# A two-layer block on one core: VectorE reads the first unit of an output-weight chunk before it makes the low part of the coming weights

## The chip, the core and the metric

The kernel runs on one core of a Trainium2 chip. The metric is the device time of one execution in microseconds, and a time for a kernel is the median of several executions. The engines are named as in the profile: PE (TensorE, matrix products), DVE (VectorE), ACT (ScalarE), POOL (GpSimd) and SP (SyncE, which here issues the loads).

## What is computed

Two blocks of two layers each are run on 256 tokens of width 1024, all in float32. Only the first block is touched. One of its layers, cut to what matters:

```python
hdn = modulate(rmsnorm(x, norm1_g[l]), shift1, scale1)
proj = hdn @ w_in[l]            # queries, keys, values of three branches, and gates
...
g_a, g_b, g_c = jnp.split(jax.nn.sigmoid(gates), N_BRANCH, axis=-1)
merged = (g_a * (o_mla @ w_o_mla[l]) + g_b * (o_sb @ w_o_sb[l])
          + g_c * (o_mb @ w_o_moba[l]))
x = x + gate1[:, None, :] * (merged @ w_out[l])
hdn = modulate(rmsnorm(x, norm2_g[l]), shift2, scale2)
ff = jnp.square(jax.nn.relu(hdn @ w_ff1[l])) @ w_ff2[l]
x = x + gate2[:, None, :] * ff
```

The three products with `w_o_sb`, `w_o_moba` and `w_o_mla` (512 x 1024 each) are what this case is about. "Output weights" means these three.

## The kernel before

**Chunks and steps.** The weights of a layer are cut into 76 chunks of up to 128 x 2048 numbers. Each engine runs one loop over the chunks (`for j in range(N_CHUNKS)`), and one turn of it is a step. The output weights have two chunks each: steps 26 and 27 (`WSB`, first branch), 32 and 33 (`WMB`, second), 38 and 39 (`WMLA`, third). Four steps of gate columns stand ahead of each pair, and steps 40 to 43 (`WOUT`) follow the last.

**Split weights.** Products are made in float32 accuracy from two parts of each operand. ScalarE makes the high part of a chunk (`split_high`, line 539, tile `w_hi`), VectorE subtracts it from the weights for the low part (`split_low`, line 545, tile `w_lo`), and TensorE does three matmuls for each pair of tiles (lines 1644, 1646 and 1648). There are two buffers for each part (`SPLIT = 2`), so in step j the chunk for step j + 2 is split, in two halves. ScalarE may write the first half once TensorE is through with the first half of the old chunk (`half_used`), and the second half once the chunk is used up (`unit_done`). The raw weights are loaded by SP into a ring of three; the load of the chunk three further waits for the low part's second half (`lo_made`).

**Units and banks.** The result of a chunk is one unit, in one of two PSUM banks (`dense`), which take turns. An output-weight chunk has two units, one for each half of its columns, with 24 matmuls each. In `products` of such a chunk, `half_used` is signalled in the second unit, at its half, hence after three quarters of the step's 48 matmuls. Before TensorE starts a unit it waits until the bank's unit before is read (`bank_of`, semaphores `evacuated`).

**Reading a unit.** VectorE multiplies a unit of an output-weight chunk by its gate (line 2209), into `merged` (tile `first_full`) for the first branch and into `gated` (tile `first_sq`) for the others. GpSimd adds `gated` to `merged` (line 2093). In the third branch ScalarE then takes the high part of the sum (line 2072) and VectorE the low part (line 2265), and the chunks of `WOUT` need both (`merged_ready`, in four pieces).

**Order on VectorE.** In a step VectorE does the attention work that is due, then the low part's first half, then `evacuate(j)`, then the low part's second half, then what is particular to the step. `split_ahead` makes the halves; for output-weight chunks each call makes one half. Instructions of an engine run in the order of its queue, and an instruction that waits holds back all behind it.

Of the kernel before, what the change touches and what calls it, by code (L numbers as in the profile page):

```python
# [13 lines left out]
ALU = mybir.AluOpType  # L14
# [34 lines left out]
GB, WSB, GC, WMB, GA, WMLA, WOUT, FF = 22, 26, 28, 32, 34, 38, 40, 44  # L49
# [76 lines left out]
def is_down(j):  # L126
    return j >= FF and FF_STEPS[j - FF][0] == "down"


def is_out(j):  # L130

    return WSB <= j < GC or WMB <= j < GA or WMLA <= j < WOUT


def units_of(j):

    if is_down(j):
        return 0
    if j == UKV:
        return 6  # L140
    return 2 if is_out(j) else 1
# [4 lines left out]
RING = [sum(units_of(i % N_CHUNKS) for i in range(g)) for g in range(DEPTH * N_CHUNKS + 1)]  # L146
DONE = [sum(max(1, units_of(i % N_CHUNKS)) for i in range(g)) for g in range(DEPTH * N_CHUNKS + 1)]
# [15 lines left out]
def constants_first():  # L163
# [16 lines left out]
    for j in range(4):  # L180
        k[32 * j, K_SEL + j] = 1.0
        for v in range(2):
# [20 lines left out]
                    gate_ready=12, merge_added=8, merged_hi=4, merged_ready=4, ff_hi_made=16, ff_ready=16,  # L203
# [44 lines left out]
def reach(engine, counted, n):  # L248
    engine.wait_ge(counted.sem, counted.left + n)
# [29 lines left out]
def layers(nc, a, keep, out):  # L279
    with ExitStack() as stack:  # L280
        m = Memory(nc, stack, "first")
# [18 lines left out]
        merged = full  # L300
        gated = sq
# [15 lines left out]
        gate = m.sb("gate", [P, KT, S])  # L317
# [31 lines left out]
        dense = [m.bank(f"dense{i}") for i in range(2)]  # L349
# [19 lines left out]
        evacuated = [m.sem(f"evacuated{i}") for i in range(2)]  # L369
# [6 lines left out]
        hi_made, lo_made, half_used, unit_done = (m.sem(n) for n in ("hi_made", "lo_made", "half_used", "unit_done"))  # L376
# [88 lines left out]
        def half_columns(g, half):  # L465

            nk, nc_ = shape_of(g % N_CHUNKS) if g < DEPTH * N_CHUNKS else (KT, CW)
            n = nk // 2 * nc_
            return slice(half * n, half * n + n)

        def split_ahead(split, g, half):


            if g < DEPTH * N_CHUNKS:
                early = half_columns(g + SPLIT, 0).stop <= half_columns(g, 0).stop and units_of(g % N_CHUNKS) <= 2
                if half and not early:
                    split(g + SPLIT, 0)
                if half or early:
                    split(g + SPLIT, half)
# [14 lines left out]
        def folds_at(at):  # L494
            return [unit for step, unit, _ in FOLDS if step == at]
# [5 lines left out]
        def groups_at(at, lag):  # L501
            return [n for n, g in enumerate(GROUPS) if GROUP_END[g] + lag == at]
# [5 lines left out]
        def pair_stage(j):  # L508

            return [(n, s) for s in (2, 1, 0) for n, at in enumerate(PAIR_STEP) if at + s * PAIR_LAG == j]  # L510
# [6 lines left out]
        for j in range(MBQ, MBV):  # L517
            t = mb_q if j < MBK else mb_k
# [1095 lines left out]
        def layer(l, next_x_ready):  # L1614

            base = l * N_CHUNKS
# [11 lines left out]
            gate_ready, merge_added, merged_hi, merged_ready = (  # L1628
                Counted(first_sems[n], FIRST_COUNTS[n] * l) for n in ("gate_ready", "merge_added", "merged_hi", "merged_ready"))
# [465 lines left out]
            def vector(dve, link):  # L2095
# [45 lines left out]
                def rope(j):  # L2141

                    t, lo, hi, kind, swap = ropes[j]
                    n, no = t.shape[1], rope_no[j]
                    wait_evacuated(dve, RING[base + j])
                    other = swapped[lo:hi, 0:n, :]
                    dve.stream_shuffle(other, t, swap).then_inc(rope_swapped.sem, 1)
                    reach(dve, rope_swapped, no + 1)
                    dve.tensor_tensor(other, other, table(kind, 1, lo, hi, n), ALU.mult)
                    link(dve.tensor_tensor(t, t, table(kind, 0, lo, hi, n), ALU.mult))  # L2150
                    dve.tensor_tensor(t, t, other, ALU.add).then_inc(rope_done.sem, 1)
                    reach(dve, rope_done, no + 1)
# [37 lines left out]
                def after_values(n):  # L2190
# [2 lines left out]
                    dve.tensor_tensor(o_lo[n // 4][:, n % 4, :], o_bank[:, 0:S], o.bitcast(F32),  # L2193
                                      ALU.subtract).then_inc(o_ready.sem, 1)

                def evacuate(j):
                    if j in ropes:
                        rope(j)
                    elif is_out(j):
                        first = {WSB: 0, WMB: 1, WMLA: 2}[j - j % 2]  # L2200
                        reach(dve, gate_ready, 4 * first + 4)
                        for e in range(2):
                            t, u = 4 * (j % 2) + 2 * e, RING[base + j] + e
                            dve.wait_ge(unit_done, DONE[base + j] + e + 1)
                            if first == 2:

                                reach(dve, merge_added, t // 2 + 1)
                            dst = gated if first else merged
                            dve.tensor_tensor(dst[:, t:t + 2, :], gate[:, t:t + 2, :],  # L2209
                                              dense[u % 2][:].rearrange("p (m t) -> p m t", m=2),  # L2210
                                              ALU.mult).then_inc(evacuated[u % 2], 1)
                    elif WOUT <= j < FF:
                        u = RING[base + j]
                        dve.wait_ge(unit_done, DONE[base + j] + 1)
                        residual(2 * (j - WOUT), dense[u % 2], 16).then_inc(evacuated[u % 2], 1)
                    elif j in UP_NO:
                        n, (_, q, c) = UP_NO[j], FF_STEPS[j - FF]
                        reach(dve, ff_hi_made, n + 1)
                        dve.tensor_tensor(ff_lo[q % 2][:, 2 * c:2 * c + 2, :], relu_sq[n % 2],
                                          ff_hi[q % 2][:, 2 * c:2 * c + 2, :].bitcast(F32),  # L2220
                                          ALU.subtract).then_inc(ff_ready.sem, 1)
                    elif is_down(j) and FF_STEPS[j - FF][1] == 3:
                        c = FF_STEPS[j - FF][2]
                        dve.wait_ge(unit_done, DONE[base + j + 1])
                        last = residual(2 * c, acc[c], 40)
                        last.then_inc(next_x_ready, 1)

                def residual(t, bank, gate_at):

                    for c in range(2):  # L2230
                        last = dve.scalar_tensor_tensor(
                            out=keep.x[:, t + c, :], in0=bank[:, c * S:(c + 1) * S],
                            scalar=mod[:, gate_at + t + c:gate_at + t + c + 1], in1=keep.x[:, t + c, :],
                            op0=ALU.mult, op1=ALU.add)
                    return last
# [10 lines left out]
                for j in range(N_CHUNKS):  # L2246
                    if j == FF:
                        norm_x(1, NORM2)
                    for n, stage in pair_stage(j):
                        (after_scores, after_second, after_values)[stage](n)  # L2250
                    for n in groups_at(base + j, SELECT_LAG):
                        keep_group(dve, n)
                    if j == WOUT:
                        dve.wait_ge(group_kept, GROUPS.index((l, "ada", 1)) + 1)
                    split_ahead(partial(split_low, dve), base + j, 0)
                    evacuate(j)
                    split_ahead(partial(split_low, dve), base + j, 1)
                    for i, at in enumerate(LAT_STEP):
                        if at <= j <= at + 2:
                            (latent_root, latent_scale, latent_low)[j - at](NORM_Q + i)  # L2260
                    if WMLA <= j < WOUT:
                        for e in range(2):
                            t = 4 * (j - WMLA) + 2 * e
                            reach(dve, merged_hi, 2 * (j - WMLA) + e + 1)
                            dve.tensor_tensor(h_lo[:, t:t + 2, :], merged[:, t:t + 2, :],
                                              h_hi[:, t:t + 2, :].bitcast(F32), ALU.subtract).then_inc(
                                                  merged_ready.sem, 1)
                    for unit in folds_at(base + j):
                        fold(dve, unit)
                    if l == DEPTH - 1:  # L2270
                        turn_vector(dve, link, j - FF, low_free)
# [5 lines left out]
        first = layer(0, later[-1]["x_ready"].sem)  # L2277
# [328 lines left out]
```

## Time and profile before

| | |
|---|---|
| median of 3 runs | 1500.1 us (1499.57 to 1501.39) |
| profiled execution, its time | 1500.05 us |
| profiled execution, its span from the first to the last instruction | 1498.2 us |
| PE busy | 1422.3 us (95%) |
| DVE busy | 839.3 us (56%) |
| ACT busy | 756.0 us (50%) |
| POOL busy | 146.2 us (10%) |
| mean granted clock of TensorE | 0.987 |

The profile is of one execution. Busy times are those of an engine's instructions; matmuls are pipelined and their ends are modelled, so they overlap each other. What counts for an engine that is nearly always busy is where it stands still, and what ended the wait.

### The profile page before, as it was taken

How to read it: one execution, taken by the hardware profiler on the slowest of the kernel's cores; microseconds unless marked ns; L12 is line 12 of the kernel's file. 1: busy time of each engine (PE TensorE's matmuls, PEld its weight loads, DVE VectorE, ACT ScalarE, POOL GpSimd, SP SyncE). 2: the span in 40 equal slices, each digit the busy share in tenths (PEclk: the TensorE clock that was granted, in tenths of full speed). 3: DMA queues.
4: the chain of work that ended last, by engine and by line, in shares of the span. 5: the costliest groups of instructions: out<-in, count | busy, mean ns of one | idle time of the engine just before them, and what ended most of it. 6: DMA issues, size and time to landing. Idle time of an engine off the chain costs nothing.

```text
span 1498.2 us, 25346 instructions
## 1 busy us (share of the span) xinstructions
PE 1422.3 (95%) x10680; PEld 1284.6 (86%) x10680; DVE 839.3 (56%) x1274; ACT 756.0 (50%) x1229; POOL 146.2 (10%) x78
## 2 busy tenths in 40 slices
PE   6999999998999998999899989999999999999988
PEld 2989878988899998998798988999998778688978
DVE  3547855546666566568845565534463635517562
ACT  3465555654545434565565554644553455425562
POOL 0000000011000000000000110000002333133321
PEclk9999999999999999999999999999999999999999
DMA  9854556454788795642755455876543221122330
GB/s 358 334 177 155 173 184 226 141 196 142 253 295 305 269 330 179 208 141 73 268 173 172 154 184 194 317 269 198 159 151 94 85 84 59 55 92 87 114 113 29
DMA packets 196292, 269.31 MB, mean 180 GB/s; under 512 B 7117, under 2 KB 175954, under 8 KB 189906
## 3 DMA queue, kind: packets, MB, share of 16 engines
q1 hardware_dynamic: 196178, 267.68, 52.4%
q8 instruction: 85, 1.39, 0.4%
q14 instruction: 29, 0.24, 0.1%
HBM read 266.61 MB, written 1.05 MB: 179 GB/s over the span
## 4 chain that ended last, share of the span: by engine, by line
PE 77%; DVE 13%; ACT 5%; issue 2%; SPq 1%; DMA 1%; DVEq 0%; ACTq 0%
PE first_dense L1644 12%; PE first_dense L1646 12%; PE first_dense L1648 12%; PE first_dense L1002 5%; PE first_dense L1005 5%; PE first_dense L1004 5%; DVE first_w_lo L545 3%; PE first_misc L228 2%; PE first_s L1644 2%; PE first_s L1646 2%; PE first_s L1648 2%; PE first_dense L1822 2%; PE first_o L1644 1%; ACT first_w_hi L539 1%; PE first_t L1644 1%
## 5 line engine op out<-in xcount | busy, mean ns | idle before, releaser
L545 DVE TENSOR_TENSOR first_w_lo<-first_raw,first_w_hi 128x1024 fp32r<-128x1024 f32 (+2 forms) x308 | 370.5, 1210 | 329.6 <-ACT first_w_hi L539 328.0
L539 ACT ACTIVATE first_w_hi<-first_raw 128x1024 fp32r<-128x1024 f32 (+2 forms) x308 | 314.9, 1029 | 273.4 <-PE first_dense L1648 128.5
L1644 PE MATMUL first_dense<-first_h_parts,first_w_hi 128*128 128x256 f32 x1312 | 376.8, 287 | 10.4 <-DVE first_sq L2209 6.5
L1646 PE MATMUL first_dense<-first_h_parts,first_w_hi 128*128 128x256 f32 x1312 | 372.5, 284 | 0.0
L1648 PE MATMUL first_dense<-first_h_parts,first_w_lo 128*128 128x256 f32 x1312 | 372.3, 284 | 0.0
L1644 PEld LDWEIGHTS first_dense<-first_h_parts,first_w_hi 128*128 128x128 f32 x1312 | 252.4, 192 | 24.0 <-issue 13.6
L1646 PEld LDWEIGHTS first_dense<-first_h_parts,first_w_hi 128*128 128x128 f32 x1312 | 252.5, 192 | 0.1
L1648 PEld LDWEIGHTS first_dense<-first_h_parts,first_w_lo 128*128 128x128 f32 x1312 | 252.5, 192 | 0.0
L702 POOL TENSOR_TENSOR first_w_lo<-first_raw,first_w_hi 128x1024 fp32r<-128x1024 f32 x41 | 100.6, 2455 | 451.3 <-ACT first_w_hi L695 451.3
L1004 PE MATMUL first_dense<-first_parts,first_w_hi 128*128 128x512 f32 (+1 forms) x384 | 130.8, 341 | 0.0
L1002 PE MATMUL first_dense<-first_h_parts,first_w_hi 128*128 128x512 f32 (+1 forms) x320 | 112.1, 350 | 0.9 <-DVE first_w_lo L702 0.9
L1005 PE MATMUL first_dense<-first_h_parts,first_w_lo 128*128 128x512 f32 (+1 forms) x320 | 109.4, 342 | 0.0
L1644 PE MATMUL first_dense<-first_parts,first_w_hi 128*128 128x256 f32 (+1 forms) x320 | 93.5, 292 | 10.0 <-ACT first_area L2012 6.5
L1648 PE MATMUL first_dense<-first_parts,first_w_lo 128*128 128x256 f32 (+1 forms) x320 | 92.1, 288 | 0.0
L1646 PE MATMUL first_dense<-first_parts,first_w_hi 128*128 128x256 f32 (+1 forms) x320 | 91.9, 287 | 0.0
L695 ACT ACTIVATE first_w_hi<-first_raw 128x1024 fp32r<-128x1024 f32 x56 | 59.0, 1056 | 60.5 <-PE first_dense L1005 60.5
L1004 PEld LDWEIGHTS first_dense<-first_parts,first_w_hi 128*128 128x128 f32 x384 | 72.8, 190 | 9.0 <-issue 1.2
L1644 PEld LDWEIGHTS first_dense<-first_parts,first_w_hi 128*128 128x128 f32 (+1 forms) x320 | 60.3, 188 | 17.6 <-issue 10.6
L1644 PE MATMUL first_s<-first_parts,first_w_hi 128*128 128x256 f32 x256 | 73.0, 285 | 0.0
L1002 PEld LDWEIGHTS first_dense<-first_h_parts,first_w_hi 128*128 128x128 f32 x320 | 60.6, 189 | 14.3 <-issue 7.8
L1646 PE MATMUL first_s<-first_parts,first_w_hi 128*128 128x256 f32 x256 | 72.4, 283 | 0.0
L1648 PE MATMUL first_s<-first_parts,first_w_lo 128*128 128x256 f32 x256 | 72.4, 283 | 0.0
(391 smaller groups left out, 2795.3 us busy)
## 6 DMA issues: line engine op xcount, KB each, us to landing
first_raw<-in_w_in SPq DMA_DIRECT2D x78, 1024.0 KB, 5.1
first_raw<-in_w_ff SPq DMA_DIRECT2D x64, 1024.0 KB, 6.4
first_units<-in_w_ada SPq DMA_DIRECT2D x41, 1024.0 KB, 6.4
first_raw<-in_w_out SPq DMA_DIRECT2D x16, 1024.0 KB, 5.1
first_mb<-in_w_mod SPq DMA_DIRECT2D x14, 1024.0 KB, 7.2
first_units<-in_w_mod SPq DMA_DIRECT2D x10, 1024.0 KB, 5.9
first_raw<-in_w_uq SPq DMA_DIRECT2D x8, 576.0 KB, 3.9
first_raw<-in_w_o_sb SPq DMA_DIRECT2D x4, 1024.0 KB, 4.9
```

Source lines behind the costliest of these rows:

```text
L228: product = pe.matmul(out[32 * j:32 * j + 32, :], c[:, t, :], moving, start=first, stop=last, skip_group_check=True)
L539: act.activation(w_hi[g % SPLIT][:, c], raw[g % CHUNK_RING][:, c], ACT.Copy).then_inc(hi_made, 1)
L545: dve.tensor_tensor(w_lo[g % SPLIT][:, c], raw[g % CHUNK_RING][:, c], w_hi[g % SPLIT][:, c].bitcast(F32), ALU.subtract).then_inc(lo_made, 1)
L695: act.activation(in_tiles(w_hi[place2(l, c, SPLIT)][:])[:, r, :], in_tiles(raw[place2(l, c, CHUNK_RING)][:])[:, r, :], ACT.Copy).then_inc( ...
L702: engine.tensor_tensor(in_tiles(w_lo[place2(l, c, SPLIT)][:])[:, r, :], in_tiles(raw[place2(l, c, CHUNK_RING)][:])[:, r, :], hi.bitcast(F3 ...
L1002: pe.matmul(out, still[0](t), moving[0](t), start=t == i == 0, stop=False, skip_group_check=True)
L1004: pe.matmul(out, still[0](t), moving[1](t), start=False, stop=False, skip_group_check=True)
L1005: last = pe.matmul(out, still[1](t), moving[0](t), start=False, stop=t == KT - 1, skip_group_check=True)
L1644: pe.matmul(out, still[0](t), moving[0](t), start=start and t == n == 0, stop=False, skip_group_check=True)
L1646: pe.matmul(out, still[0](t), moving[1](t), start=False, stop=False, skip_group_check=True)
L1648: last = pe.matmul(out, still[1](t), moving[0](t), start=False, stop=stop and t == nk - 1, skip_group_check=True)
L1822: pe.matmul(at[i][:, c, :], part[:, t, c * P:(c + 1) * P], h_hi[:, t, :], start=part is w[i][0] and t == c == 0, stop=False, skip_group_ch ...
```

## The change

In the steps of output weights the reads of the two units are taken apart. The read of the first unit (`evacuate_out(j, 0)`, with its waits) comes ahead of the low part of the first half of the chunk two steps ahead, and the read of the second unit (`evacuate_out(j, 1)`) stays between the two halves. The rest of `evacuate` is as it was.

```diff
+                def evacuate_out(j, e):
+                    first = {WSB: 0, WMB: 1, WMLA: 2}[j - j % 2]
+                    t, u = 4 * (j % 2) + 2 * e, RING[base + j] + e
+                    reach(dve, gate_ready, 4 * first + 4)
+                    dve.wait_ge(unit_done, DONE[base + j] + e + 1)
+                    if first == 2:
+                        reach(dve, merge_added, t // 2 + 1)
+                    dst = gated if first else merged
+                    dve.tensor_tensor(dst[:, t:t + 2, :], gate[:, t:t + 2, :],
+                                      dense[u % 2][:].rearrange("p (m t) -> p m t", m=2),
+                                      ALU.mult).then_inc(evacuated[u % 2], 1)
+
                 def evacuate(j):
                     if j in ropes:
                         rope(j)
-                    elif is_out(j):
-                        first = {WSB: 0, WMB: 1, WMLA: 2}[j - j % 2]
-                        reach(dve, gate_ready, 4 * first + 4)
-                        for e in range(2):
...
+
+                    if is_out(j):
+                        evacuate_out(j, 0)
                     split_ahead(partial(split_low, dve), base + j, 0)
+                    if is_out(j):
+                        evacuate_out(j, 1)
                     evacuate(j)
                     split_ahead(partial(split_low, dve), base + j, 1)
```

## Rows read from the trace of the kernel before

**Rows 1.** The page, part 1: busy us, share of the span, instructions.

```profile
PE 1422.3 (95%) x10680; PEld 1284.6 (86%) x10680; DVE 839.3 (56%) x1274; ACT 756.0 (50%) x1229; POOL 146.2 (10%) x78
```

**Rows 2.** Line 2209: durations in ns, min/median/max; who waited (us, times).

```profile
L2209 DVE TENSOR_TENSOR first_sq<-first_gate,first_dense x16: 678/680/682, 295.9 to 887.1; 128x512 f32<-128x512 f32 x16
...
  PE first_dense L1644: 8.2, 6
```

**Rows 3.** Timeline of TensorE: start us, duration us, instruction, idle before and releaser.

```profile
259.21 0.39 PE L1644 MATMUL first_dense<-first_h_parts,first_w_hi 128*128 128x256 f32 x1 [0.84 <-DVE first_full L2209]
...
302.37 0.28 PE L1648 MATMUL first_dense<-first_parts,first_w_lo 128*128 128x256 f32 x1
...
304.28 0.39 PE L1644 MATMUL first_dense<-first_h_parts,first_w_hi 128*128 128x256 f32 x1 [1.63 <-DVE first_sq L2209]
...
336.01 0.35 PE L1644 MATMUL first_dense<-first_parts,first_w_hi 128*128 128x256 f32 x1 [1.68 <-issue]
...
343.63 0.39 PE L1644 MATMUL first_dense<-first_h_parts,first_w_hi 128*128 128x256 f32 x1 [1.64 <-DVE first_sq L2209]
...
347.87 0.36 PE L1644 MATMUL first_dense<-first_h_parts,first_w_hi 128*128 128x256 f32 x1 [1.10 <-DVE first_h_parts L2265]
...
701.33 0.80 PE L1785 MATMUL first_o<-first_small,first_area 128*64 128x256 f32 x2 [2.13 <-DVE first_small L2187]
...
891.48 0.36 PE L1644 MATMUL first_dense<-first_h_parts,first_w_hi 128*128 128x256 f32 x1 [1.10 <-DVE first_h_parts L2265]
```

**Rows 4.** Chain of waits, 300 to 306 us: start, us on the chain, what.

```profile
301.31 1.07 ACT first_w_hi L539
...
302.40 0.04 DVE first_w_lo L545
...
303.55 0.69 DVE first_sq L2209
...
304.28 0.39 PE first_dense L1644
```

**Rows 5.** Timeline of VectorE, first and second branch.

```profile
257.34 1.23 DVE L545 TENSOR_TENSOR first_w_lo<-first_raw,first_w_hi 128x1024 fp32r<-128x1024 f32 x1 [4.16 <-ACT first_w_hi L539]
...
302.40 1.23 DVE L545 TENSOR_TENSOR first_w_lo<-first_raw,first_w_hi 128x1024 fp32r<-128x1024 f32 x1 [2.99 <-ACT first_w_hi L539]
```

**Rows 6.** Timelines of VectorE, GpSimd and ScalarE, third branch.

```profile
334.08 1.23 DVE L545 TENSOR_TENSOR first_w_lo<-first_raw,first_w_hi 128x1024 fp32r<-128x1024 f32 x1 [1.25 <-ACT first_w_hi L539]
...
335.99 3.53 POOL L2093 TENSOR_TENSOR first_full<-first_full,first_sq 128x512 f32<-128x512 f32 x2 [28.15 <-DVE first_sq L2209]
...
339.55 0.63 ACT L2072 ACTIVATE first_h_parts<-first_full 128x512 fp32r<-128x512 f32 x1 [1.60 <-POOL first_full L2093]
...
340.21 0.69 DVE L2265 TENSOR_TENSOR first_h_parts<-first_full,first_h_parts 128x512 fp32r<-128x512 f32 x1
...
341.75 1.23 DVE L545 TENSOR_TENSOR first_w_lo<-first_raw,first_w_hi 128x1024 fp32r<-128x1024 f32 x1 [0.85 <-ACT first_w_hi L539]
...
343.65 1.29 POOL L2093 TENSOR_TENSOR first_full<-first_full,first_sq 128x512 f32<-128x512 f32 x1 [4.14 <-DVE first_sq L2209]
...
344.09 1.94 DVE L545 TENSOR_TENSOR first_w_lo<-first_raw,first_w_hi 128x1024 fp32r<-128x1024 f32 x1
...
344.90 2.27 POOL L2093 TENSOR_TENSOR first_full<-first_full,first_sq 128x512 f32<-128x512 f32 x1
...
345.95 1.77 DVE L2265 TENSOR_TENSOR first_h_parts<-first_full,first_h_parts 128x512 fp32r<-128x512 f32 x1
```

**Rows 7.** Stretches: length; busy us and instructions of PE, PEld, DVE, ACT, POOL; PEclk; DMA share; GB/s.

```profile
337.00:348.00 11.00, 8.26 (x67) 7.89 (x66) 9.86 (x9) 4.81 (x7) 6.03 (x4) 1.00 0.38 112
...
450.00:580.00 130.00, 128.27 (x1050) 121.95 (x1050) 82.16 (x72) 59.57 (x71) 0.00 (x0) 1.00 0.85 297
...
586.00:590.00 4.00, 4.00 (x24) 4.00 (x24) 4.00 (x11) 2.50 (x7) 0.00 (x0) 0.62 0.02 6
...
700.00:704.00 4.00, 2.37 (x9) 1.37 (x10) 3.19 (x7) 3.63 (x6) 0.47 (x1) 0.71 0.00 0
```

More of the change, by code:

```diff
@@ L2198, in evacuate @@
                         rope(j)
-                    elif is_out(j):
-                        first = {WSB: 0, WMB: 1, WMLA: 2}[j - j % 2]
-                        reach(dve, gate_ready, 4 * first + 4)
-                        for e in range(2):
[L2203 to L2211, printed above, removed]
                     elif WOUT <= j < FF:
```

## Prediction

> **What bounds the kernel.** The page's first part is read first: TensorE is busy for 1422.3 of 1498.2 us [rows 1], so a change pays only where TensorE stands still. Next comes the list of what line 2209, the read of an output-weight unit, is waited for by: TensorE waited 8.2 us for it, in six pauses [rows 2]. TensorE's timeline then places the pauses. In the first layer they end at 259.21 (0.84 us), 304.28 (1.63), 336.01 (1.68, put down to "issue", but it ends as the first of two reads finishes) and 343.63 (1.64); the second layer repeats them 543.6 us later, as the row at 891.48 does for the one at 347.87 [rows 3]. That last one (1.10 us) waits for the low part of the merged result (line 2265).
>
> The chain of waits through one pause tells its cause. TensorE finishes the third quarter of the step's products; only then may ScalarE take the high part of the first half of the weights two steps ahead (301.31, 1.07 us); VectorE takes the low part (302.40); then it reads the first unit (303.55), and TensorE goes on at 304.28 [rows 4]. The first unit's products had been ready since half of the step. TensorE needs its bank, not the weights, which are for two steps later.
>
> **What the change removes and adds.** No instruction is added or removed, and no DMA. In twelve steps (three pairs in each of two layers) one multiply of 0.68 us [rows 2] goes ahead of one subtraction of 1.23 us. The wait for the gates goes forward too (they are done a step earlier), and in the third branch the wait for the second branch's sums (GpSimd was done with them 28.15 us earlier [rows 6]). The second read keeps its place before the second subtraction, which can start up to 0.68 us earlier; SP's next load of weights waits for that one, and is so no later.
>
> *The wait moved forward.* VectorE now stops at the queue's head for unit one, at half of the step, where it used to stop for ScalarE after three quarters. It stood idle before that subtraction for 4.16 us in the step at 257, 2.99 at 302, 1.25 at 334 and 0.85, the shortest of the twelve, at 341 [rows 5, 6]. So the 0.68 us fits into idle time everywhere and the subtraction keeps its time; that cover is gone only in the step at 341, once TensorE comes earlier (below). Without cover it costs 0.68 us of VectorE, in front of a low part that TensorE wants a step and a half later: nothing on the path.
>
> *Pairs of the first branch (two in the kernel).* The first of their steps is followed by attention work and row products on TensorE, so its bank is free in time either way: 0. The second: VectorE stands idle for 4.16 us ahead of 257.34 [rows 5], in which the unit comes ready and is read, so the bank is free before it is asked for, and the pause of 0.84 us goes but for the usual handover of 0.05: 0.8 us.
>
> *Pairs of the second branch.* In the first step the transposes behind it nearly hide the read; I take 0.15 us (bounds 0 and 0.3). The second step's pause goes whole. A pause counted from a modelled end of a matmul (start 302.37 plus 0.28) is short by what matmuls overlap: they start 0.12 us apart (1050 in 127 to 130 us [rows 7]), so 0.16 is added, and 304.28 moves to 302.49: 1.79 us. The next chunks' low parts are done by then: the second half's was made one step before.
>
> *Pairs of the third branch.* The first step's pause goes: 1.68 + 0.16 = 1.84 us, so the second step starts at 334.17. There a second chain takes over, and I walk it [rows 6]. GpSimd adds each read to the sum (line 2093). Its add takes 1.29 us alone at 343.65, while VectorE reads a bank beside it at no cost; but VectorE's subtraction issued at 344.09 takes 1.94 us instead of 1.23, which is 1.23 us counted from the add's end; GpSimd's next add (344.90) takes 2.27, which is about 1.14 from the subtraction's end; the subtraction of line 2265 issued at 345.95 then takes 1.77 instead of 0.69. So subtractions and adds take turns whole. The Trainium skill, "SBUF — State Buffer", section "Who interferes with whom", states this as a lock: a VectorE instruction with two SBUF inputs and a GpSimd one that reads SBUF block each other for the whole instruction, and one with a single SBUF input doesn't contend; the trace agrees.
>
> With the change the first read comes right behind the work that ends 1.25 us ahead of 334.08: 332.8 to 333.5. The first add starts then, and the subtraction at 334.08 waits for it until 334.7, ending at 335.95. Second read to 336.55, second subtraction (now ahead of the add) to 337.70, add to 338.9, ScalarE's high part to 339.55 (as before), line 2265 to 340.28 instead of 340.90. Then the first read of the second step, 340.20 to 340.88: TensorE, done with that step at 340.15, starts the next chunk at 340.94 instead of 343.63. First subtraction to 342.03, second read to 342.63, add 342.03 to 343.2, second subtraction to 344.35, add to 345.5, line 2265 to 346.05: TensorE passes its last pause at 346.2 instead of 347.87. So of 1.84 + 1.80 + 1.26 us, 1.7 us are gained and the rest is the same wait in a later place. Bounds: if GpSimd's third add gets in ahead of the subtraction at 340.8, 0.9 us later, gain 0.8; if line 2265 gets in ahead of the last add, 1.15 us earlier, gain 2.8. I take 1.7: the subtraction is asked for 0.1 us before the add.
>
> **Sum.** Per layer 0.8 + 0.15 + 1.79 + 1.7 = 4.44 us; two layers 8.9. The profiled execution took 1500.05 us, 1.85 more than its span, and the median of the three runs is 1500.1, the same. 1500.1 - 8.9 = 1491.2 us.
>
> Behind these places everything is released by TensorE's own progress: the feed-forward stretch from 450 to 580 us keeps TensorE busy 128.27 of 130 us with the DMA engines 85% busy [rows 7], and its loads are issued as splits finish, so they move along.
>
> **Rivals.** *The third branch gives nearly all back.* GpSimd and VectorE take turns in the bad order there, and more often than in my walk. For it: requests only 0.1 us apart. Against it: even the bad order, once, leaves 0.8; with half of that, 2 x (0.8 + 0.15 + 1.79 + 0.4) = 6.3, so 1493.8 us. 0.13.
>
> *The clock falls in the longer pause.* The pauses of 1.10 to 1.68 us left the granted clock at 1.00 from 337 to 348 us. The one of 2.13 us that ends at 701.33 [rows 3] was followed by 0.50, which leaves 0.71 as the mean of 700 to 704, and 586 to 590 has 0.62 [rows 7]: half of 2.4 GHz. My new pause before 346.2 is about 2.3 us. A mean of 0.62 over 4 us is 3.0 us at 0.50, so a fall gives back 1.5 us. The Trainium skill, "TensorE: Matmul & The Clock Gate", Part 1, has the clock at only these two levels and lets it fall when the engine has been idle; the trace shows both levels. Once: 1492.7; in both layers: 1494.2. 0.27 together. It can go the other way too, since pauses further on shift and the one at 701 might keep its clock: 1489.7.
>
> *DMA takes it back.* If the feed-forward stretch were paced by the DMA engines, TensorE would wait there for what it gained, and the first layer's 4.4 us would be lost: 1495.7, or 1499 with a like loss in the second. Against it: TensorE's 98.7% there. 0.06.
>
> *Slower: the head of the queue.* If VectorE, stopped for unit one or for the merge before it, delays the low part of weights two steps ahead until TensorE wants it, each of twelve steps pays 0.68 us: 8.2 us, 1508. It decides from the point where the low part is late by more than the step between making and use, over 5.8 us (48 matmuls at 0.12); idle time of 0.85 to 4.16 us in front of it says it is far off. 0.03.
>
> **How the numbers follow.** The sum as forecast has 0.51 (its own range 1490 to 1492.5); the rivals have 0.13, 0.27, 0.06 and 0.03. From 1488.8 (the good order of locks in both layers) to 1495.2 holds all but the DMA rival, the slow one and tails. A measurement of this kernel can tell 0.2%, 3 us, from no change: all cases but the last two are faster by more, and a part of DMA's is the same. Faster 0.92, same 0.05, slower 0.03.
>
> **What would show it.** In the changed profile VectorE's line for the read stands singly, one before each first subtraction; the pauses near 259 and 304 are gone (TensorE's next chunk starts 0.12 us after the last matmul); near 336 none, near 341 one below 1 us, near 344 one of some 2 us on line 2265. GpSimd's first add lies beside the first subtraction, which reads 1.8 us. The granted clock behind that pause decides the clock rival; a new wait of ScalarE for a load, with a pause of TensorE behind it in 380 to 580, the DMA one. I am wrong if TensorE's pauses outside these steps grow by what is gained here.

## The result, and the profile after

| | before | changed |
|---|---|---|
| median of 6 runs each | 1500.02 us (1499.43 to 1501.39) | 1492.39 us (1491.34 to 1496.47) |
| profiled execution: time, span, mean granted clock | 1500.05, 1498.2 us, 0.987 | 1496.47, 1494.7 us, 0.983 |

The ratio is 0.995 with a 95% interval of 0.994 to 0.996: 7.6 us less. The profiled execution of the changed kernel is the slowest of its six, so its own rows add up to 3.6 us. Places along its timeline are therefore compared one by one. They show 7.3 us gained in the touched steps of the two layers, and 1.1 us lost ahead of them, 1.7 between 907 and 917 us, and 1.0 behind 1452.

TensorE's timeline of the changed kernel, at the places of [rows 3]:

```profile
259.35 0.36 PE L1644 MATMUL first_dense<-first_h_parts,first_w_hi 128*128 128x256 f32 x1
...
302.30 0.28 PE L1644 MATMUL first_dense<-first_h_parts,first_w_hi 128*128 128x256 f32 x1
...
338.73 0.39 PE L1644 MATMUL first_dense<-first_h_parts,first_w_hi 128*128 128x256 f32 x1 [0.73 <-DVE first_sq L2204]
...
343.86 0.35 PE L1644 MATMUL first_dense<-first_h_parts,first_w_hi 128*128 128x256 f32 x1 [1.99 <-DVE first_h_parts L2269]
```

The pauses at 259 and 304 are gone, the one at 336 too; 0.73 us stands in place of the 1.64 at 343.63; and the last one, for the merged result's low part, has grown from 1.10 to 1.99 us. Just ahead of the touched steps the times are 1.12 us later than in the profile of before (0.92 of it arises in the first 40 us), so a place's gain is its shift against that: the chunk behind the first branch starts 0.98 us earlier (259.35 for 259.21), the one behind the second branch 3.10 (302.30 for 304.28), and the last pause ends 5.13 earlier (343.86 for 347.87).

VectorE, GpSimd and ScalarE of the changed kernel, third branch (to [rows 6]; line 2204 is the read, line 2269 what was 2265):

```profile
330.66 0.68 DVE L2204 TENSOR_TENSOR first_sq<-first_gate,first_dense 128x512 f32<-128x512 f32 x1
...
331.42 1.30 POOL L2093 TENSOR_TENSOR first_full<-first_full,first_sq 128x512 f32<-128x512 f32 x1 [25.09 <-DVE first_sq L2204]
...
332.00 1.80 DVE L545 TENSOR_TENSOR first_w_lo<-first_raw,first_w_hi 128x1024 fp32r<-128x1024 f32 x1 [0.66 <-ACT first_w_hi L539]
...
334.32 1.21 DVE L545 TENSOR_TENSOR first_w_lo<-first_raw,first_w_hi 128x1024 fp32r<-128x1024 f32 x1
...
334.48 2.21 POOL L2093 TENSOR_TENSOR first_full<-first_full,first_sq 128x512 f32<-128x512 f32 x1 [1.76 <-DVE first_sq L2204]
...
336.72 0.64 ACT L2072 ACTIVATE first_h_parts<-first_full 128x512 fp32r<-128x512 f32 x1 [2.79 <-POOL first_full L2093]
```

The read stands singly ahead of the first subtraction, and GpSimd's first add now lies under that subtraction, which takes 1.80 us. Turn by turn it is the order of the prediction's walk; the walk's times are 2.1 us later at its start and 2.3 us later at its end.

Stretches of the changed kernel (columns as in [rows 7]), behind that last pause in each layer, and one further on:

```profile
344.60:347.60 3.00, 3.00 (x16) 3.00 (x16) 1.23 (x1) 0.17 (x1) 0.00 (x0) 0.50 0.79 269
884.20:887.20 3.00, 3.00 (x16) 3.00 (x16) 1.55 (x2) 0.54 (x1) 0.00 (x0) 0.51 0.86 286
908.00:911.00 3.00, 3.00 (x9) 2.34 (x8) 0.10 (x1) 0.92 (x2) 0.00 (x0) 0.50 0.00 0
```

The granted clock is 0.50 for some 3 us behind the pause of 1.99 us, in both layers: 16 matmuls start in 3 us where the kernel before starts 25 at clock 1.00 in the stretches behind the same wait:

```profile
347.90:350.90 3.00, 3.00 (x25) 3.00 (x26) 1.88 (x2) 0.88 (x1) 0.00 (x0) 1.00 0.95 308
891.50:894.50 3.00, 3.00 (x25) 3.00 (x26) 1.90 (x2) 0.90 (x1) 0.00 (x0) 1.00 0.93 305
```

The next chain, the squares behind `WOUT`, begins at 367.47 for 369.97. Of the 5.13 us, 3.62 are left, so the fall costs 1.51 us; in the second layer it costs 1.46. The third stretch is a fall that the kernel before didn't have there, behind a pause of 1.73 us that follows TensorE's last matmuls of `WOUT`.

### The profile page after: what moved, and what is told of

The parts are those of the page before. It is cut to its first block, busy times and chain, and to the rows that moved or that the text cites. A ratio compares the mean times of both kernels' runs of the same rounds, so it can differ in the third digit from the quotient of the medians.

```text
span 1494.7 us, 25354 instructions
## 1 busy us (share of the span) xinstructions
PE 1425.7 (95%) x10680; PEld 1287.4 (86%) x10680; DVE 837.0 (56%) x1274; ACT 755.5 (51%) x1229; POOL 147.8 (10%) x78
## 4 chain that ended last, share of the span: by engine, by line
PE 78%; DVE 13%; ACT 5%; issue 2%; SPq 1%; DMA 1%; POOL 0%; DVEq 0%; ACTq 0%
PE first_dense L1644 12%; PE first_dense L1646 12%; PE first_dense L1648 12%; PE first_dense L1002 5%; PE first_dense L1005 5%; PE first_dense L1004 5%; DVE first_w_lo L545 3%; PE first_misc L228 2%; PE first_s L1644 2%; PE first_dense L1822 2%; PE first_s L1648 2%; PE first_s L1646 2%; PE first_o L1644 1%; PE first_t L1644 1%; PE first_o L1648 1%
```

## Experiments

The theory was: what is gained are the waits for banks; in the third branch a new wait of about 2 us stands behind them, and the clock falls because of it. Every kernel ran beside the kernel before. A ratio is of the kernel's time to that of before in the same session, whose median was 1500.55 us in the first (first four kernels) and 1501.06 us in the second, on another chip. The changed kernel itself ran in the first only, so kernels of the second are compared with it by their ratios.

### The changed kernel again

> The changed kernel once more, beside the others of this call. Theory (TensorE's pauses for banks go; in the third branch a longer pause comes in their place, and the granted clock falls behind it in some executions): 6 to 9 us less than before, about 1492.5 against 1500, with the single times spread over 4 us or so. Rival (the spread has nothing to do with the third branch's pause): the same median, and kernels without that pause spread as widely.

1493.71 us (1488.54 to 1496.67), ratio 0.9952 (0.9936 to 0.9967). Its last pauses are 1.99 us again, and the clock behind them is 0.50 again (0.51 and 0.50 in the first profile). So both profiled executions of this kernel have the fall in both layers; whether every execution has it isn't shown.

```profile
343.90:346.90 3.00, 3.00 (x16) 3.00 (x15) 1.22 (x1) 0.18 (x1) 0.00 (x0) 0.50 0.77 267
883.40:886.40 3.00, 3.00 (x16) 3.00 (x16) 1.64 (x2) 0.64 (x1) 0.00 (x0) 0.50 0.87 296
```

### Only the first and second branch

```diff
-                    if is_out(j):
+                    if is_out(j) and j < WMLA:
                         evacuate_out(j, 0)
                     split_ahead(partial(split_low, dve), base + j, 0)
+                    if is_out(j) and not (j < WMLA):
+                        evacuate_out(j, 0)
```

> The first unit is read early in the first and second branch only; the third branch keeps the old order. Theory: TensorE's starts in the changed profile say 1.0 us (first branch), 0.3 and 1.9 us (second) per layer, so 2 x 3.2 = 6.4 us less than before, 1493.6, and no fall of the clock near 340 and 885. Rival (the third branch brings nearly nothing in the end, as its pauses move and the clock falls): this kernel is as fast as the full change or faster, within 1 us. Rival (branches are not independent, the gain comes mostly from the third): less than 3 us.

1493.86 us (1489.83 to 1496.05), ratio 0.9954 (0.9943 to 0.9966): 6.7 us less than before, near the 6.4 of the theory's sum, and the same as the full change, as the first rival says. Both hold: the first two branches bring what their places say, and the third adds nothing that the medians can show. The last pause is 1.09 us as before the change, with no fall behind it:

```profile
344.86 0.36 PE L1644 MATMUL first_dense<-first_h_parts,first_w_hi 128*128 128x256 f32 x1 [1.09 <-DVE first_h_parts L2271]
```
```profile
344.90:347.90 3.00, 3.00 (x25) 3.00 (x26) 1.88 (x2) 0.89 (x1) 0.00 (x0) 1.00 0.95 304
882.60:885.60 3.00, 3.00 (x25) 3.00 (x26) 1.88 (x2) 0.89 (x1) 0.00 (x0) 1.00 0.94 309
```

The times spread over 6.2 us here too, so the spread isn't tied to the third branch's pause; on this point the theory was wrong. The profile shows one source of it. Further on, behind the same pause of 3.21 us, this execution has the full clock and the changed kernel's has half:

```profile
582.37 0.35 PE L1822 MATMUL first_dense<-first_h_parts,first_w_hi 128*128 128x256 f32 x1 [3.21 <-ACT first_h_parts L1940]
```
```profile
582.40:585.40 3.00, 3.00 (x25) 3.00 (x26) 3.00 (x9) 3.00 (x8) 0.00 (x0) 1.00 0.00 0
```
```profile
582.86 0.35 PE L1822 MATMUL first_dense<-first_h_parts,first_w_hi 128*128 128x256 f32 x1 [3.21 <-ACT first_h_parts L1940]
```
```profile
583.40:586.40 3.00, 3.00 (x16) 3.00 (x15) 3.00 (x8) 2.59 (x7) 0.00 (x0) 0.50 0.00 0
```

The first two are of this kernel, the last two of the changed one. From there to the pause of 2.13 us near 697 us this kernel is 3.0 us faster, though the change touches nothing there.

### Only the third branch

The same edit with `j >= WMLA` in place of `j < WMLA`, twice.

> The first unit is read early in the third branch only. Theory: 1.9 us per layer is gained at TensorE's last pause, which then is about 2.0 us long; if the granted clock falls behind it (0.5 for some 3 us) 1.5 us of that is given back in that layer. So 3.8 us less than before if it falls in neither layer (1496.2), 0.8 us less if in both (1499.2). Rival (the fall in the profile was chance and not tied to the longer pause): 3.8 us less, clock 1.00 near 345 and 888.

1501.48 us (1499.10 to 1502.93, 11 runs), ratio 1.0006 (0.9997 to 1.0014). The pause is 1.99 us, and the clock falls behind it in both layers (0.61 and 0.53 in the stretches of 3 us):

```profile
346.19 0.36 PE L1644 MATMUL first_dense<-first_h_parts,first_w_hi 128*128 128x256 f32 x1 [1.99 <-DVE first_h_parts L2271]
```
```profile
346.20:349.20 3.00, 3.00 (x17) 3.00 (x18) 1.91 (x2) 0.91 (x1) 0.00 (x0) 0.61 0.94 308
889.40:892.40 3.00, 3.00 (x15) 3.00 (x16) 1.83 (x2) 0.83 (x1) 0.00 (x0) 0.53 0.93 303
```

Its timeline gives 1.95 us gained at the last pause of the first layer (346.19 for 347.87, with 0.27 us lost before the steps) and 0.45 us left at the squares (369.79 for 369.97). The rival without a fall, 3.8 us less, is out. The expected 0.8 us less (0.9995) lies just outside the interval. The profile has the 0.4 us that are left in each layer, and loses 1.7 us between 1087 and 1361 us, where nothing was changed: its mean clock is 0.84 from 1085 to 1096 us, that of before 1.00. Such a loss outweighs what is left.

### TensorE kept busy in the pause

```diff
+                        if first is not None and t == 4:
+                            for _ in range(16):
+                                pe.matmul(t_bank[1][:, 0:S], outs[0][1][0](4), outs[0][2][0](0), start=True, stop=True)
                         if first is not None:
                             reach(pe, *first(t))
```

> The changed kernel with 16 more matmuls of 256 columns on TensorE in each layer, at the place of its last pause (ahead of the wait for the third piece of the merged result); their result goes to an unused bank. TensorE has as much to wait for as before, only it isn't idle meanwhile. Theory (the clock falls because of the pause): pause of about 0.1 us, granted clock 1.00 behind it, so up to 2 x 1.5 us less than the changed kernel: 1490 to 1491, and a narrower spread. Rival (the clock has nothing to do with it, the pause alone costs): the same time as the changed kernel, or up to 0.5 us more.

1490.88 us (1488.48 to 1493.14), ratio 0.9938 (0.9926 to 0.9949): 2.8 us less than the changed kernel of the same session, with 32 matmuls more. The intervals of the two overlap in 0.9936 to 0.9949, so the times alone don't settle it. The profile does: no pause, clock 1.00 at the place of the falls, and at the squares 1.5 us more gained in the first layer than in the changed kernel's (364.56, from a start 0.26 us earlier than in the profile of before).

```profile
340.32 2.08 PE L1642 MATMUL first_t<-first_h_parts,first_w_hi 128*128 128x256 f32 x16
```
```profile
340.00:343.00 3.00, 2.99 (x26) 2.78 (x25) 2.85 (x3) 1.40 (x3) 1.80 (x1) 1.00 0.34 71
878.00:881.00 3.00, 2.98 (x25) 2.78 (x24) 2.71 (x3) 1.50 (x2) 1.72 (x2) 1.00 0.46 104
```

TensorE had to wait for as much as in the changed kernel, and only was not idle meanwhile. So the fall comes from the idleness, not from the work behind it.

### The merged result ahead of the weights

```diff
                     if is_out(j):
                         evacuate_out(j, 0)
+                    if j == WMLA + 1:
+                        evacuate_out(j, 1)
+                        merged_low(j)
                     split_ahead(partial(split_low, dve), base + j, 0)
-                    if is_out(j):
+                    if is_out(j) and j != WMLA + 1:
                         evacuate_out(j, 1)
```

`merged_low` is the loop of line 2265 as a function; in step 38 it keeps its place.

> The changed kernel, and in the last step of the third branch VectorE does both reads and the low parts of the merged result (line 2265) ahead of both low parts of weights. Theory (what is left of the pause is VectorE's and GpSimd's turns, with the weights' low parts ahead of line 2265, and the clock falls only because the pause is about 2 us): line 2265 ends 1.8 us earlier, TensorE's last pause shrinks from 1.99 to about 0.2 us, no fall of the clock near 344 and 884; 2 x (1.8 + 1.5) = 6.6 us less than the changed kernel, about 1486.5. Rival (the low part of the next chunk's weights is then late, and a pause of the same length stands one chunk further): a pause of over 1 us near 347 and 888, and 1490 or more.

1485.78 us (1485.39 to 1490.11), ratio 0.9907 (0.9894 to 0.9921); the theory said 1486.5. Of the last pause next to nothing is left (the chunk's fifth tile starts at 340.53, 0.41 us after the matmul before it, where matmuls otherwise start 0.12 us apart), the clock stays at 1.00, and no pause for a low part stands behind it, although VectorE comes to the weights only at 341.14:

```profile
337.27 0.39 PE L1644 MATMUL first_dense<-first_h_parts,first_w_hi 128*128 128x256 f32 x1 [0.72 <-DVE first_sq L2204]
...
340.12 0.28 PE L1648 MATMUL first_dense<-first_h_parts,first_w_lo 128*128 128x256 f32 x1
...
340.53 0.36 PE L1644 MATMUL first_dense<-first_h_parts,first_w_hi 128*128 128x256 f32 x1
```
```profile
340.00:343.00 3.00, 2.87 (x24) 2.69 (x23) 2.86 (x4) 1.56 (x2) 0.00 (x0) 1.00 0.02 5
877.00:880.00 3.00, 2.87 (x24) 2.80 (x24) 2.86 (x4) 1.26 (x2) 0.00 (x0) 1.00 0.00 0
```

### Both reads ahead of the weights

```diff
                     if is_out(j):
                         evacuate_out(j, 0)
+                        evacuate_out(j, 1)
                     split_ahead(partial(split_low, dve), base + j, 0)
-                    if is_out(j):
-                        evacuate_out(j, 1)
```

> The changed kernel with the second unit's read, too, ahead of the low part of the first half of weights, in all twelve steps. VectorE's queue is then held for the end of the step's products. Theory (the low part has over a step of slack, as the prediction says): TensorE's pauses of the first and second branch stay gone, only the third branch's last pause gets longer by up to 0.5 us a layer: 0 to 1 us more than the changed kernel. Rival (waiting at the queue's head is what costs, and the change only just escapes it): pauses for the low part (line 545) behind steps 27, 33 or 39, and 3 us or more over the changed kernel.

1494.44 us (1492.22 to 1496.35), ratio 0.9956 (0.9943 to 0.9968), the changed kernel's within the interval. VectorE waits at the head of its queue for the end of the step's products, and no pause of TensorE for line 545 stands behind steps 27, 33 or 39. The third branch's last pause is 0.25 us longer and the one before it shorter (0.25 us for 0.73). The low parts have their slack, and the slower rival's mechanism is out by more than the change asks for.

```profile
341.84 0.36 PE L1644 MATMUL first_dense<-first_h_parts,first_w_hi 128*128 128x256 f32 x1 [2.24 <-DVE first_h_parts L2268]
```

### The third branch's adds on VectorE

```diff
-                    if WMB <= j < GA or WMLA <= j < WOUT:
+                    if WMB <= j < GA:
...
-                        reach(dve, merge_added, t // 2 + 1)
+                        reach(dve, merge_added, 4)
...
+                    if first == 2:
+                        wait_evacuated(dve, u)
+                        dve.tensor_tensor(merged[:, t:t + 2, :], merged[:, t:t + 2, :], gated[:, t:t + 2, :],
+                                          ALU.add).then_inc(merge_added.sem, 1)
```

> The changed kernel with the third branch's four adds per layer (line 2093) on VectorE behind each read, none on GpSimd. Theory (VectorE and GpSimd take turns whole, so an add of 1.29 us on GpSimd costs VectorE 0.6 to 1.1 us each time): VectorE's instructions there go back to 1.23 and 0.69 us; line 2265 ends 0.8 us earlier although VectorE has four more instructions of 0.69 us; the pause keeps its length of about 1.9 us and the clock falls as before: 1.6 us less than the changed kernel, about 1491.5. Rival (the turns cost nothing, VectorE is bound by its own work): 2.0 us more, since VectorE has 4 x 0.69 us more to do in each layer.

1488.72 us (1487.19 to 1489.93), ratio 0.9918 (0.9904 to 0.9932): more than the theory gave (0.9943), far from the rival's 2.0 us more. At the last pause TensorE is 1.3 us a layer ahead of the changed kernel, not 0.8, and the fall of 1.5 us is spared besides. VectorE's subtraction under the first add is back at its own length although VectorE has the adds to do as well:

```profile
331.43 0.69 DVE L2209 TENSOR_TENSOR first_full<-first_full,first_sq 128x512 f32<-128x512 f32 x1
332.05 1.23 DVE L545 TENSOR_TENSOR first_w_lo<-first_raw,first_w_hi 128x1024 fp32r<-128x1024 f32 x1
```

What the expectation had wrong is the clock: the pause is 1.67 us, not 1.9, and behind it the clock stays at 1.00. The pause of 0.73 us ahead of it is gone too, so this kernel alone doesn't tell which of the two keeps the clock; in *Both reads ahead of the weights* the clock fell with only 0.25 us left there.

```profile
342.60 0.36 PE L1644 MATMUL first_dense<-first_h_parts,first_w_hi 128*128 128x256 f32 x1 [1.67 <-DVE first_h_parts L2273]
```
```profile
342.60:345.60 3.00, 3.00 (x25) 3.00 (x26) 1.59 (x2) 0.00 (x0) 0.00 (x0) 1.00 0.81 228
878.40:881.40 3.00, 3.00 (x25) 3.00 (x26) 1.59 (x2) 0.00 (x0) 0.00 (x0) 1.00 0.80 230
```

### Both edits: adds on VectorE, merged result first

> The two edits before together: adds on VectorE, and in the last step of the third branch the reads, adds and low parts of the merged result ahead of the weights' low parts. Theory: the bank is free 0.7 us earlier and line 2265 is in time, so both pauses of the third branch are gone: 0.7 us a layer less than with the order alone, about 1485; no fall of the clock near 344 and 884. Rival (weights' low parts come late): a pause for line 545 one chunk further, and no better than with the order alone.

1481.85 us (1480.99 to 1483.23), ratio 0.9874 (0.9860 to 0.9887): 19.2 us less than before, 3.9 less than with the order alone. In this profile TensorE has no pause of 0.6 us or more from 250 to 361 us, and its clock is 1.00 there:

```profile
338.00:341.00 3.00, 3.00 (x27) 3.00 (x27) 2.87 (x4) 1.69 (x3) 0.00 (x0) 1.00 0.17 56
874.00:877.00 3.00, 3.00 (x27) 3.00 (x27) 3.00 (x5) 1.06 (x1) 0.00 (x0) 1.00 0.44 117
```

This is the fastest of the kernels, faster than both of the case. Over the order alone its places gain 1.3 us a layer, 2.7 in both, where 0.7 a layer was expected. The profiles also differ where the edits touch nothing: behind the pause of 3.21 us that ends at 576.58 this one keeps the full clock, the order alone has half, and up to the pause of 2.13 us near 690 it is 3.0 us faster for it.

```profile
576.60:579.60 3.00, 3.00 (x25) 3.00 (x26) 3.00 (x9) 3.00 (x8) 0.00 (x0) 1.00 0.01 3
```
```profile
578.60:581.60 3.00, 3.00 (x16) 3.00 (x15) 3.00 (x8) 2.58 (x7) 0.00 (x0) 0.50 0.00 0
```

How much of the remaining 1.2 us between the medians is such clock isn't shown.

## Why the prediction was right

**The place and the cause of the pauses: right.** TensorE's pauses for banks went where VectorE's first read came forward, in all steps named, and nothing else was lost there: TensorE has no pause of 0.6 us or more between 376 and 574 us, and the squares at 367.47 and the pause that ends at 582.86 are both 2.5 us earlier than before, so the DMA rival is out. That the first read fits into VectorE's idle time held, and *Both reads ahead of the weights* shows slack beyond it.

**The terms of the sum**, per layer, read off as above: first branch 0.98 us for 0.8; second 2.12 (3.10 less 0.98) for 1.94; third 2.03 (5.13 less 3.10) for 1.7. In all 5.13 for 4.44. The first was small because the group's column products before it overlap with the next chunk as other matmuls do, which the prediction added in the other branches and forgot here. The second was small because the first step's pause, put at 0.15 us, is worth 0.33 (the second step ends at 302.30 less 1.12 instead of 302.49, less the 0.98 of the first branch). In the third, VectorE's second subtraction got its turn ahead of the last add, as in the walk; the first read came 0.16 us sooner than the walk has it, and the turns behind it took 0.2 us less in all.

**The step that failed** is the choice between the forecast and one of its rivals, *the clock falls in the longer pause*. The rival had 0.27 and is what the profiles show: in all six places, two in each of three profiles, with a pause of 1.99 us (the change twice, the third branch alone), and in the two with 2.24 (both reads first). The forecast put the pause at 2.3 us and still gave its own case, full clock, 0.51. The cost was 1.5 us a layer, as priced from [rows 7]. With measured terms and the fall, 2 x (5.13 - 1.5) = 7.3 us, 1492.8; measured 7.6. The forecast of 1491.2 was near by luck: terms 1.4 us too small and 3.0 us of clock left out partly cancel, so 1492.39 lies within the 1490 to 1492.5 of a case that the profiles don't show. By the rival's own number, both falls, it would have been 1494.2.

**The third branch's part** is therefore worth next to nothing as it stands: some 0.4 us a layer by the places, which the medians can't show. The kernel without it is as fast (0.9954 and 0.9952), the kernel with it alone is no faster than before (1.0006). The rival that the third branch gives nearly all back named the wrong taker, the turns of VectorE and GpSimd; those fell as in the walk, and the clock took it.

**Smaller sums.** The lower bound, the good order in both layers, comes to 1500.1 - 2 x (0.8 + 0.15 + 1.79 + 2.8) = 1489.0, not 1488.8; the DMA rival with a like loss in both layers to 1500.1, not 1499; and no sum of the prediction gives 1495.2.

## What to carry to other kernels

When a wait is taken out of a chain, look for the next one on it and add up its new length: three short pauses of 1.1 to 1.7 us cost only themselves, while one of 2.0 us cost itself and 1.5 us more of half clock. Filling such a pause with useless products gained 2.8 us. By the ratios, putting the waited-for work ahead of work with slack gained 6.8 us over the changed kernel, moving GpSimd's adds to VectorE, with which they took turns, gained 5.1, and both together 11.7.

## What the runs showed of the hardware

Pauses inside TensorE's dense stream of 0.7 to 1.7 us left the granted clock at 1.00 (1.63 to 1.68 before the change, 1.67 with the adds on VectorE); those of 1.99 to 2.24 us at this place were followed by 0.50 for some 3 us, in eight of eight places. The Trainium skill, "TensorE: Matmul & The Clock Gate", Part 1, has the clock drop to half when the engine has been idle. The trace agrees as to the half, and in these eight places as to the idleness: 16 matmuls start in 3 us at 0.50 and 25 at 1.00.

Elsewhere the clock isn't settled by the pause's length. A pause of 3.21 us near 580 us left it at 1.00 in two profiles (the first two branches only, and both edits) and was followed by 0.50 in the two shown beside them. Behind the same pause of 1.73 us, near 907 to 914 us, the changed kernel's profile has 0.50 and the one before 1.00, which is worth 1.7 us between the same two places (907.41 to 917.03 against 913.60 to 921.52). What decides it there isn't shown. Executions of one kernel spread over up to 8 us (1488.54 to 1496.67), those of the kernel before over 3.6.

In the third branch of the changed kernel GpSimd's adds and VectorE's subtractions took turns whole, as before the change (subtractions of 1.80 and 1.72 us for 1.23 alone, an add of 2.21 for 1.29). With the adds on VectorE, a layer's four cost it 4 x 0.69 us, and the last of the chain came 1.3 us earlier all the same.
